# Expert 0's rows from a gather of six tiles and one-hot products of two, in a hybrid decoder layer with 32 experts

## The chip, the core and the metric

The kernel runs on one core of a Trainium2 chip. The metric is the device time of one execution, in microseconds. The engines are PE (TensorE, matrix products), DVE (VectorE), ACT (ScalarE), POOL (GpSimd) and SP (SyncE, which here only issues transfers). Each follows its own list of instructions in order; they meet at semaphores. The transfers of SP, ACT and POOL run on 16 shared DMA engines.

## The reference

The layer mixes tokens by a convolution group and an attention group, then runs a mixture of experts. The change is at the seam of the two:

```python
x = x + jnp.concatenate([yc, ya], axis=-1) @ w_out
xn = rms_norm(x, norm_ffn_w)
g_idx = argmax(xn @ w_group + b_group)            # 1 of 4 groups
top_v, top_i = top_k(e_logits of that group, 2)   # 2 of its 8 experts
# per expert e, over the tokens routed to it, in blocks:
h = silu(xb @ w1[e]) * (xb @ w3[e])
y = h @ w2[e]
x = x + sum over the token's two experts of gate * y
```

There are 1024 tokens of width 1024 and 32 experts of inner width 512. All is float32.

## The kernel before

**Tiles and stages.** The 1024 tokens are 8 tiles of 128, numbered m = 0 to 7. In the last loop of the mixing part PE multiplies tile m by `w_out` (`multiply`, halves h = 0 and 1 of 512 columns, eight chunks each), DVE adds the residual (`add(m, h)`), PE turns the sum (`turn`), ACT or DVE copies it out of PSUM, and PE multiplies it by the router's 36 columns (`route`). DVE then picks group and experts (`bias`, `choose_group`, `choose_experts`), PE counts how many earlier tokens chose each expert (`count_before`), and DVE makes from the count each token's slot in its expert's list (`rank`). `one_hots` on DVE and `table` on PE turn slots into a table of which token stands in which slot of which expert, by 16 products of one-hot matrices. DVE reads it with `slots`, which gives `slot_token`. Routing runs in groups of tiles: 0 to 3, 4 and 5, 6, 7. Normalised rows `xn2` of each tile are stored to DRAM by SP.

**Experts.** POOL gathers the rows of an expert, up to 128, from DRAM to `xg` (two buffers) by an indirect transfer. PE turns them (`pe_turn_x`; for expert 0 `first_turn_x`). ACT writes the rounded half `xT_hi`, DVE the rest `xT_lo`. Each weight matrix (`W1`, `W3`, `W2`: 2.1 MB each, two buffers of each, [0] for even experts and [1] for odd) is split the same way in four pieces: ACT writes `e_hi` (`act_split`), DVE `e_lo` (`dve_split`), and PE makes three products per chunk of the piece (`pe_product`). Six products of 512 columns belong to a piece, so 24 to a matrix. The order on PE for expert e is gate(e) with W1, the turn of the hidden values of e-1, up(e) with W3, the turn of the rows of e+1, down(e-1) with W2. Called "W3 of expert 2" below is the matrix that up(2) needs, in buffer `W3[0]`.

**What sets the order.** All orders are written out by hand. SP issues W3 of expert 0 when the last `multiply` is done, W1 of expert 1 when the first gather has landed, then W3 of expert 1, W2 of expert 0, W1 of expert 2, W2 of expert 1, and W3 of expert 2 when the split of W3 of expert 0 is done. Tokens over 128 for an expert go to a list of overflow blocks (`flag_blocks`, `list_blocks`, `listed`, `over_ready`), worked off at the end. Between the routing and the first expert PE runs 34 transposes whose result nobody reads (L1532, L1536).

## Time and profile before

| | us |
|---|---|
| median of 3 runs | 1164.63 |
| lowest, highest | 1163.91, 1165.25 |
| the profiled execution, its own time | 1164.24 |
| its span in the profile | 1162.1 |

| engine | busy us | share of the span |
|---|---|---|
| PE | 1096.3 | 94% |
| DVE | 900.1 | 77% |
| ACT | 718.6 | 62% |
| POOL | 139.7 | 12% |

The profile lists when each instruction started and what it waited for. The profiled execution took 0.39 us less than the median; its span leaves out 2.1 us around the work. The mixing part fills the span up to 530 us, the experts fill it from 550 us to some 1120 us, and the end reads the experts' results back and adds them.

### The profile page before, as it was taken

What the parts mean: (1) busy time and instruction counts of PE and PEld (TensorE: products, weight loads), DVE (VectorE), ACT (ScalarE), POOL (GpSimd) and SP (SyncE); (2) the same over time, 40 slices, a digit from 0 to 9 for tenths busy, and PEclk for the clock granted to TensorE, in tenths of its full rate; (3) what the DMA queues carried; (4) which work ended last, traced back from release to release, by engine and by line L of the source; (5) the groups of instructions that cost most, each with busy time, mean ns of one, the idle gap of its engine ahead of it and who ended that gap; (6) DMA issues with size and microseconds to landing.
All of it is one profiled execution on the core that took longest, in us unless ns stands there. A gap on an engine that the chain in (4) does not pass through costs nothing. (4 is left out here: it accounts for less than half of the span.)

```text
span 1162.1 us, 16798 instructions
## 1 busy us (share of the span) xinstructions
PE 1096.3 (94%) x5766; PEld 894.9 (77%) x5766; DVE 900.1 (77%) x1033; ACT 718.6 (62%) x882; POOL 139.7 (12%) x192
## 2 busy tenths in 40 slices
PE   8999999999999899997999999999999999999950
PEld 7887777778777668885878888888888888888840
DVE  5505957678575772567989999999999999999947
ACT  5423555646643571112878888888888888888830
POOL 1001000010000120001021110111111111101000
PEclk9999999999999999997999999999999999999985
DMA  7111231313213253003999999999999999999529
GB/s 232 46 35 39 90 89 59 107 39 107 67 46 95 103 214 142 37 37 133 425 427 422 396 384 396 386 384 396 382 383 390 382 392 383 390 387 387 214 77 375
DMA packets 77117, 275.29 MB, mean 237 GB/s; under 512 B 20752, under 2 KB 51600, under 8 KB 63888
## 3 DMA queue, kind: packets, MB, share of 16 engines
q1 hardware_dynamic: 66272, 253.69, 57.6%
q0 software_dynamic: 9216, 16.80, 3.8%
q10 hardware_dynamic: 1584, 4.20, 0.9%
q8 instruction: 29, 0.48, 0.2%
q14 instruction: 16, 0.13, 0.0%
HBM read 259.57 MB, written 31.85 MB: 251 GB/s over the span
## 5 line engine op out<-in xcount | busy, mean ns | idle before, releaser
L1198 DVE TENSOR_TENSOR e_lo<-W,e_hi 128x1024 fp32r<-128x1024 f32 x384 | 451.9, 1219 | 24.5 <-ACT e_hi L1192 21.7
L1192 ACT ACTIVATE e_hi<-W 128x1024 fp32r<-128x1024 f32 x384 | 403.4, 1060 | 94.7 <-PE ps L1163 88.7
L1161 PE MATMUL ps<-e_hi,xT_hi 128*128 128x512 f32 x496 | 196.3, 396 | 1.9 <-DVE xT_lo L1920 1.0
L1163 PE MATMUL ps<-e_lo,xT_hi 128*128 128x512 f32 x496 | 193.7, 390 | 0.0
L1162 PE MATMUL ps<-e_hi,xT_lo 128*128 128x512 f32 x496 | 193.1, 389 | 0.0
L472 PE MATMUL ps<-xnT_hi,w_hi 128*128 128x512 f32 x320 | 129.0, 403 | 1.6 <-DVE u L861 0.6
L472 PE MATMUL ps<-xnT_hi,w_lo 128*128 128x512 f32 x320 | 128.0, 400 | 0.0
L472 PE MATMUL ps<-xnT_lo,w_hi 128*128 128x512 f32 x320 | 125.3, 392 | 0.0
L900 DVE TENSOR_TENSOR_SCAN kept<-kept,start_at 128x1024 f32<-128x1024 f32 (+7 forms) x64 | 88.9, 1389 | 29.1 <-ACT kept L702 29.1
L1161 PEld LDWEIGHTS ps<-e_hi,xT_hi 128*128 128x128 f32 x496 | 93.5, 189 | 20.9 <-DVE xT_lo L1920 1.2
L1163 PEld LDWEIGHTS ps<-e_lo,xT_hi 128*128 128x128 f32 x496 | 93.1, 188 | 19.9
L1162 PEld LDWEIGHTS ps<-e_hi,xT_lo 128*128 128x128 f32 x496 | 93.3, 188 | 18.4
L1161 PE MATMUL ps<-e_hi,hidT_hi 128*128 128x512 f32 x256 | 102.4, 400 | 1.6 <-DVE hidT_lo L1232 1.6
L1163 PE MATMUL ps<-e_lo,hidT_hi 128*128 128x512 f32 x256 | 100.0, 390 | 0.0
L1162 PE MATMUL ps<-e_hi,hidT_lo 128*128 128x512 f32 x256 | 99.9, 390 | 0.0
L1259 POOL DMA_INDIRECT y_rows<-y,idx_pair x32 | 35.2, 1101 | 455.3 <-ACT y L1219 455.3
L711 ACT ACTIVATE probsT<-ps 128x512 f32<-128x512 f32 (+3 forms) x60 | 28.0, 504 | 84.1 <-PE ps L521 84.1
L472 PEld LDWEIGHTS ps<-xnT_hi,w_hi 128*128 128x128 f32 x320 | 60.1, 188 | 19.2 <-issue 7.1
L472 PEld LDWEIGHTS ps<-xnT_hi,w_lo 128*128 128x128 f32 x320 | 60.1, 188 | 13.0 <-issue 0.7
L472 PEld LDWEIGHTS ps<-xnT_lo,w_hi 128*128 128x128 f32 x320 | 60.1, 188 | 12.2 <-issue 0.5
L702 ACT ACTIVATE kept<-ps,q_minus 128x1024 f32<-128x1024 f32 (+7 forms) x64 | 47.8, 746 | 32.7 <-PE ps L510 32.6
L405 POOL CAST w_hi<-w_raw 128x1024 fp32r<-128x1024 f32 x20 | 22.4, 1120 | 301.4 <-DMA w_raw<-in_w_in_dram 301.4
(244 smaller groups left out, 1706.9 us busy)
## 6 DMA issues: line engine op xcount, KB each, us to landing
W<-in_w_dram SPq DMA_DIRECT2D x96, 2048.0 KB, 15.2
w_raw<-in_w_in_dram SPq DMA_DIRECT2D x20, 512.0 KB, 4.1
yy<-y_rows SPq DMA_DIRECT2D x7, 1024.0 KB, 12.7
xt<-in_x_dram SPq DMA_DIRECT2D x8, 512.0 KB, 3.7
w_out_raw<-in_w_out_dram SPq DMA_DIRECT2D x8, 512.0 KB, 6.4
xn_rows<-xn SPq DMA_DIRECT2D x8, 512.0 KB, 2.6
out_dram<-x ACTq DMA_DIRECT2D x7, 512.0 KB, 9.1
x<-in_x_dram SPq DMA_DIRECT2D x2, 1536.0 KB, 10.7
```

The lines of the kernel that those rows point to most:

```text
L405: pool.tensor_copy(w_hi[c % 2], w_raw[c % 2]).then_inc(w_hi_made, 1)
L472: mm = pe.matmul(ps[:, group_bank(g)], w, r, start=(i % TICKS == 0), stop=(i % TICKS == TICKS - 1))
L702: act.activation(kept[h][:, S - L:], z, ACT.Sigmoid, scale=down).then_inc(kept_made, 1)
L711: act.activation(probsT[h][:, k0:k1, :], TB(th(n, h) + hf)[:, 0:(k1 - k0) * P].rearrange("p (k t) -> p k t", t=P), ACT.Copy).then_inc(turn ...
L900: dve.tensor_tensor_scan(back, back, one[:, ::-1], 0.0, ALU.mult, ALU.max).then_inc(multiplied, 1)
L1161: pe.matmul(o, xs_hi[:, k], e_hi[:, p, cols], start=(k == 0), stop=False)
L1162: pe.matmul(o, xs_lo[:, k], e_hi[:, p, cols], start=False, stop=False)
L1163: mm = pe.matmul(o, xs_hi[:, k], e_lo[:, p, cols], start=False, stop=(k == last))
L1192: act.activation(e_hi[:, p], flat[:, p * D:(p + 1) * D], ACT.Copy).then_inc(s["hi_made"], 1)
L1198: dve.tensor_tensor(e_lo[:, p], flat[:, p * D:(p + 1) * D], e_hi[:, p], ALU.subtract).then_inc(s["lo_made"], 1)
L1259: pool.indirect_dma_start(out=y_rows, out_offset=bass.IndirectOffsetOnAxis(ap=idx_pair[b].bitcast(U32), axis=0), in_=y[b], in_offset=None, ...
```

## The change

Expert 0 no longer waits for the whole table. Four things are done:

1. **Expert 0's rows.** `rank` also makes `first_code`, a token's place in expert 0's list plus one, or zero. `first_one_hots` makes from it a one-hot matrix for each tile (`HOT(m)`). For tiles 0 to 5 `first_list` multiplies these by the tokens' numbers, and POOL gathers the rows named while tile 7 is still multiplied. ACT and DVE split the rows (`first_hi`, `first_lo`), and `first_gathered` turns them by products with the identity `eye`. For tiles 6 and 7 no row is gathered: `first_added` multiplies the normalised rows, still in SBUF, by the tile's one-hot matrix into the same PSUM banks. `first_turn_x` and the 34 unread transposes are gone.
2. **Weights of expert 0's gate.** W1 of expert 0 is split during tiles 5 to 7 into buffers of its own, `e0_hi` and `e0_lo`.
3. **The last half tile.** The second half of tile 7 is added, turned, copied and routed as two parts of 256 columns (`add_last`, `turn_last`, `route_last`). Its second `scale_last` now stands ahead of `bias`.
4. **Order behind.** The last four products of the table stand inside the gate of expert 0, ahead of its last piece. The overflow list stands inside up(0), and the turn of expert 1's rows behind up(0). SP issues W1 of expert 1 right behind the last store of rows, and W3 of expert 1 once expert 1's rows have been gathered.

The core of the diff:

```diff
+HOT = lambda m: first_hot[:, m] if m < NT - 2 else last_hot[:, m - NT + 2]
+first_hi = at("first_hi", 136, [P, D], F32R)
...
-def act_split(act, s, start, w, pieces=range(PIECES)):
+def act_split(act, s, start, w, pieces=range(PIECES), hi=e_hi, free=False):
...
+        if not free:
+            act.wait_ge(s["freed"], start + p + 1)
+        act.activation(hi[:, p], flat[:, p * D:(p + 1) * D], ACT.Copy).then_inc(s["hi_made"], 1)
...
@@ -1333,8 +1351,8 @@
                 sp.dma_start(W3[0], w3_v[0]).then_inc(expert_w[0][1], 16)
             sp.wait_ge(xn2_made, m + 1 if m < NT - 1 else NT + 1)
             sp.dma_start(xn2_rows_v[m], xn2[m % 2]).then_inc(xn2_stored[m % 2], 16)
-        sp.wait_ge(s_e["gathered"][0], 16)
         sp.dma_start(W1[1], w1_v[1]).then_inc(expert_w[1][0], 16)
+        sp.wait_ge(s_e["gathered"][1], 16)
         sp.dma_start(W3[1], w3_v[1]).then_inc(expert_w[1][1], 16)
...
+        sp.wait_ge(s_e["freed"], used(gate_start(0) + PIECES))
         load(W1, w1_v, 2, 0, 0, gate_start(0))
...
         for b in range(2):
-            pool.wait_ge(xn2_stored[b], 16 * (NT // 2))
+            pool.wait_ge(xn2_stored[b], 16 * (NT // 2 - 1))
+        pool.wait_ge(first_listed, 1)
+        gather_rows(pool, xg[0], first_token, s_e["gathered"][0], S - 2 * P)
+        pool.wait_ge(xn2_stored[0], 16 * (NT // 2))
+        pool.wait_ge(xn2_stored[1], 16 * (NT // 2))
         pool.wait_ge(routed, 1)
-        for e in range(2):
-            gather_rows(pool, xg[e], slot_token[:, e:e + 1], s_e["gathered"][e])
+        gather_rows(pool, xg[1], slot_token[:, 1:2], s_e["gathered"][1])
         pool_gather(pool, s_e, 2, 0, 1, 1, 2)
         pool_gather_start(pool, s_e, 0, 1)
...
+        def turn_last():
+            for q in range(2):
+                pe.wait_ge(x2_made, 2 * NT + q)
+                pe.wait_ge(x2T_made, 2 * NT - 2 + q)
+                for k in range(2):
+                    c = 4 + 2 * q + k
+                    mm = pe.transpose(ps[:, 5 - q, k * P:(k + 1) * P], x2[:, X2(NT - 1), c * P:(c + 1) * P], ident)
+                mm.then_inc(x2_turned, 1)
...
+        def route_last():
+            for q in range(2):
+                pe.wait_ge(x2T_made, 2 * NT + q)
+                for k in range(4 + 2 * q, 6 + 2 * q):
+                    mm = pe.matmul(ps[:, 6, P:P + LOG], x2T[1][:, k], router_w[:, k], start=False, stop=(k == KT - 1))
...
+        def first_list():
+            bank, c0 = FIRST_AT
+            pe.wait_ge(iotas, 12)
+            pe.wait_ge(first_hots, NT - 2)
+            for m in range(NT - 2):
+                mm = pe.matmul(ps[:, bank, c0:c0 + 2], first_hot[:, m], token_less[:, m:m + 2], start=(m == 0), stop=(m == NT - 3))
+            mm.then_inc(first_summed, 1)
...
+        def first_gathered(h):
...
+                pe.wait_ge(rows0_lo_made, 1)
+                pe.wait_ge(x2_made, 2 * NT + 1)
+            for k in range(4 * h, 4 * h + 4):
+                o = psf[:, k * P:(k + 1) * P]
+                pe.matmul(o, first_hi[:, k:D:KT], eye, start=(k % 4 == 0), stop=False)
+                pe.matmul(o, first_lo[:, k:D:KT], eye, start=False, stop=False)
+
+        def first_added(m, ks):
+            if ks[0] == 0:
+                pe.wait_ge(first_hots, m + 1)
+                pe.wait_ge(xn2_made, m + 1 + (m == NT - 1))
+            for k in ks:
+                mm = pe.matmul(psf[:, k * P:(k + 1) * P], xn2[m % 2][:, k:D:KT], HOT(m), start=False, stop=(m == NT - 1 and k % 4 == 3))
+                if m == NT - 1 and k % 4 == 3:
+                    mm.then_inc(s_e["turned"] if k == KT - 1 else half_turned, 1)
...
+            if m == 7:
+                first_list()
...
             multiply(pe, m, 1, (4, 5))
-            if m == 7:
-                route(7, 0)
-                count_before(2)
-            multiply(pe, m, 1, (6, 7))
             if m == 6:
                 count_before(1)
...
+            if m == 7:
+                count_before(2)
+                route(7, 0)
+            multiply(pe, m, 1, (6, 7))
...
+        turn_last()
+        first_gathered(0)
+        route_last()
+        first_gathered(1)
+        first_added(NT - 2, range(0, KT - 1))
         count_before(3)
         count_all()
-        table(12, 16)
-        for i in range(20):
-            pe.transpose(ps[:, 4, 0:P], ident, ident)
-        pe.wait_ge(listed, 1)
-        pe.matmul(ps[0:1, 3, 0:P], over_col, ident, start=True, stop=True).then_inc(list_turned, 1)
-        for i in range(14):
-            pe.transpose(ps[:, 4, 0:P], ident, ident)
...
+        first_added(NT - 2, (KT - 1,))
+        first_added(NT - 1, range(KT))
...
             pe.wait_ge(half_lo_made, 1)
-            pe_product(pe, s_e, 0, xT_hi, xT_lo, [ps[:, 2]], 2, KT - 1, (0, 1))
+            pe_product(pe, s_e, 0, xT_hi, xT_lo, [ps[:, 2]], 2, KT - 1, (0, 1), **own)
             pe.wait_ge(s_e["xT_made"], 1)
-            pe_product(pe, s_e, 0, xT_hi, xT_lo, [ps[:, 2]], 2, KT - 1, (2, 3))
+            pe_product(pe, s_e, 0, xT_hi, xT_lo, [ps[:, 2]], 2, KT - 1, (2,), **own)
+            table(12, 16)
+            pe_product(pe, s_e, 0, xT_hi, xT_lo, [ps[:, 2]], 2, KT - 1, (3,), **own)
...
+                pe_product(pe, s_e, up_start(0), xT_hi, xT_lo, [ps[:, 3]], 2, KT - 1, (0, 1))
+                overflow_list()
+                pe_product(pe, s_e, up_start(0), xT_hi, xT_lo, [ps[:, 3]], 2, KT - 1, (2, 3))
+                pe_turn_x(pe, s_e, 1, 1, 1)
+                return
+            if isinstance(e, int) and e == 1:
                 pe.wait_ge(over_ready, 1)
-                pe_turn_x(pe, s_e, 1, 1, 1)
...
+                if m == NT - 2:
+                    act.wait_ge(s_e["gathered"][0], 16)
+                    act.activation(first_hi, xg[0], ACT.Copy).then_inc(rows0_hi_made, 1)
...
+                    act.wait_ge(y_lo_made, Y_PARTS)
+                    act.wait_ge(expert_w[0][0], 16)
+                    act_split(act, s_e, gate_start(0), W1[0], hi=e0_hi, free=True)
...
+            act_split(act, s_e, up_start(e), W3[b], free=isinstance(e, int) and e == 0)
             if isinstance(e, int) and e == 0:
+                act.wait_ge(s_e["freed"], used(gate_start(0) + PIECES))
                 act_xT(act, s_e, 1)
...
+        def add_last():
+            dve.wait_ge(mixed, 2 * NT)
+            for q in range(2):
+                cols = slice(BANK // 2 * q, BANK // 2 * (q + 1))
+                part = x2[:, X2(NT - 1), BANK:][:, cols]
+                dve.tensor_tensor(part, MB(NT - 1, 1)[:, cols], part, ALU.add).then_inc(x2_made, 1)
...
+        def first_one_hots(first, last):
+            for m in range(first, last):
+                dve.tensor_scalar(HOT(m), iota[:, 1:P + 1], first_code[:, m:m + 1], None, ALU.is_equal).then_inc(first_hots, 1)
...
+            link(dve.scalar_tensor_tensor(first_code[:, ms], earlier[:, :, 0], 1.0, chosen[:, ms, 0], ALU.add, ALU.mult))
+            if i == 3:
+                first_one_hots(NT - 1, NT)
...
-                rank(1)
                 one_hots(8, 12)
+                dve.wait_ge(first_summed, 1)
+                dve.tensor_scalar(first_token, ps[:, FIRST_AT[0], FIRST_AT[1]:FIRST_AT[1] + 1], 2.0 * S, None, ALU.add).then_inc(first_listed, 1)
+                dve_split(dve, s_e, gate_start(0), W1[0], (2,), hi=e0_hi, lo=e0_lo)
...
                 choose_experts(1)
+                rank(1)
+                first_one_hots(4, 6)
             if m == 7:
                 choose_experts(2)
+                dve.wait_ge(rows0_hi_made, 1)
+                dve.tensor_tensor(first_lo, xg[0], first_hi, ALU.subtract).then_inc(rows0_lo_made, 1)
                 rank(2)
-            add(m, 1)
+                first_one_hots(6, 7)
+            if m == NT - 1:
+                add_last()
...
+            if m == 6:
+                dve_split(dve, s_e, gate_start(0), W1[0], (1,), hi=e0_hi, lo=e0_lo)
...
-
-        dve.wait_ge(x2_turned, 2 * NT)
-        dve.tensor_copy(x2T[1][:, 4:8].rearrange("p k t -> p (k t)"), ps[:, 5]).then_inc(x2T_made, 1)
-        one_hots(12, 14)
+            if m == 5:
+                first_one_hots(0, 4)
+                dve_split(dve, s_e, gate_start(0), W1[0], (0,), hi=e0_hi, lo=e0_lo)
...
+        for q in range(2):
+            dve.wait_ge(x2_turned, 2 * NT + q)
+            dve.tensor_copy(x2T[1][:, 4 + 2 * q:6 + 2 * q].rearrange("p k t -> p (k t)"), ps[:, 5 - q, 0:BANK // 2]).then_inc(x2T_made, 1)
         invert(NT - 1)
         scale_last(0)
+        scale_last(1)
         bias(NT - 1)
         choose_group(3)
         choose_experts(3)
-        scale_last(1)
         rank(3)
+        one_hots(12, 14)
+        first_x_lo()
+        dve_split(dve, s_e, gate_start(0), W1[0], (3,), hi=e0_hi, lo=e0_lo)
         one_hots(14, 16)
-        dve.wait_ge(table_step, HOTS)
-        slots(slice(0, NE))
...
             if isinstance(e, int) and e == 0:
-                dve_split(dve, s_e, gate_start(0), W1[0], (2, 3))
+                dve_split(dve, s_e, up_start(0), W3[0], (0, 1))
+                pick_blocks()
+                dve_split(dve, s_e, up_start(0), W3[0], (2,))
+                list_blocks()
+                dve_split(dve, s_e, up_start(0), W3[0], (3,))
                 make_gates()
-            elif not (isinstance(e, int) and e == 1):
-                dve_split(dve, s_e, gate_start(e), W1[b])
-            dve_split(dve, s_e, up_start(e), W3[b])
-            if isinstance(e, int) and e == 0:
+                dve_split(dve, s_e, gate_start(1), W1[1], (0,))
                 dve_xT(dve, s_e, 1)
-                dve_split(dve, s_e, gate_start(1), W1[1], (0, 1))
+                dve_split(dve, s_e, gate_start(1), W1[1], (1,))
                 dve_hid(dve, s_e, 0, up_start(0))
                 dve_split(dve, s_e, gate_start(1), W1[1], (2, 3))
...
+        ask_gates()
         flag_blocks()
+        dve.wait_ge(table_step, HOTS)
+        slots(slice(0, NE))
```

**PE, from the counts of tile 7 to the first product of an expert.** Before:

```order
L1481 MATMUL ps<-chosen,ones 128x32 x7
L1486 MATMUL ps<-chosen,ones 128x32 x8
L1492 MATMUL ps<-of_column_162,of_slot_158 128x256 [waits hot]
L1492 MATMUL ps<-of_column_163,of_slot_159 128x256 [waits hot]
L1492 MATMUL ps<-of_column_164,of_slot_160 128x256 [waits hot]
L1492 MATMUL ps<-of_column_165,of_slot_161 128x256 [waits hot]
L1532 MATMUL ps<-start_at 128x128 x20
L1534 MATMUL ps<-start_at,over_col 1x128 [waits listed]
L1536 MATMUL ps<-start_at 128x128 x14
L1542 MATMUL ps<-start_at,xg_183 128x128 [waits first_gathered0]
L1542 MATMUL ps<-start_at,xg_183 128x128 x7
L1161 MATMUL ps<-e_hi,xT_hi 128x512 [waits first_lo_made,half_lo_made]
```

After (`xn_0`, `xn_1` are the normalised rows of tiles 6 and 7):

```order
L1553 MATMUL ps<-eye,first_lo 128x128
L1560 MATMUL ps<-last_hot,xn_0_96 128x128 [waits xn2_made,first_hots]
L1560 MATMUL ps<-last_hot,xn_0_96 128x128 x6
L1521 MATMUL ps<-chosen,before 128x32 [waits chosen_made,iotas]
L1523 MATMUL ps<-chosen,ones 128x32 x7
L1528 MATMUL ps<-chosen,ones 128x32 x8
L1560 MATMUL ps<-last_hot,xn_0_96 128x128
L1560 MATMUL ps<-last_hot,xn_1_97 128x128 [waits xn2_made,first_hots]
L1560 MATMUL ps<-last_hot,xn_1_97 128x128 x7
L1179 MATMUL ps<-e_hi,xT_hi 128x512 [waits first_lo_made,half_lo_made]
```

The table's products, the unread transposes, the overflow list and the turn of gathered rows are gone from this place; 15 products with the one-hot matrices of tiles 6 and 7 stand there, around the counts. The eight of tile 7 wait for its one-hot matrix.

**PE, between gate(0) and gate(1), around the turn of expert 1's rows.** Before, the turn stands between gate(0) and up(0):

```order
L1163 MATMUL ps<-e_lo,xT_hi 128x512
L1150 MATMUL ps<-start_at,xg_184 128x128 [waits first_xT_made,first_gathered1,over_ready]
L1150 MATMUL ps<-start_at,xg_184 128x128 x7
L1161 MATMUL ps<-e_hi,xT_hi 128x512 [waits first_lo_made,first_hidden]
L1162 MATMUL ps<-e_hi,xT_lo 128x512
```

After, it stands between up(0) and gate(1):

```order
L1181 MATMUL ps<-e_lo,xT_hi 128x512
L1168 MATMUL ps<-start_at,xg_188 128x128 [waits first_xT_made,first_gathered1]
L1168 MATMUL ps<-start_at,xg_188 128x128 x7
L1179 MATMUL ps<-e_hi,x1T_hi 128x512 [waits first_lo_made,first_silu,first_xT_made]
L1180 MATMUL ps<-e_hi,x1T_lo 128x512
```

The product behind the turn needs, in the order before, rows that were turned long ago (`xT_hi`), and in the new order the very rows just turned (`x1T_hi`).

**SP, weights from the last `multiply` on.** `W_0_102` is buffer W1[0], `W_0_104` W3[0], `W_0_106` W2[0]; `W_1_103`, `W_1_105` and `W_1_107` are W1[1], W3[1] and W2[1]. Before:

```order
L1333 DMA W_0_104<-in_w_dram 128x4096 [waits mixed]
L1335 DMA xn_rows<-xn_1_97 128x1024 [waits xn2_made]
L1337 DMA W_1_103<-in_w_dram 128x4096 [waits first_gathered0]
L1338 DMA W_1_105<-in_w_dram 128x4096
L1341 DMA W_0_106<-in_w_dram 128x4096 [waits list_turned,listed]
L1346 DMA W_0_102<-in_w_dram 128x4096 [waits first_lo_made]
L1350 DMA W_1_107<-in_w_dram 128x4096
L1346 DMA W_0_104<-in_w_dram 128x4096 [waits first_lo_made]
```

After:

```order
L1351 DMA W_0_104<-in_w_dram 128x4096 [waits mixed]
L1353 DMA xn_rows<-xn_1_97 128x1024 [waits xn2_made]
L1354 DMA W_1_103<-in_w_dram 128x4096
L1356 DMA W_1_105<-in_w_dram 128x4096 [waits first_gathered1]
L1359 DMA W_0_106<-in_w_dram 128x4096 [waits list_turned,listed]
L1364 DMA W_0_102<-in_w_dram 128x4096 [waits first_lo_made,first_freed]
L1369 DMA W_1_107<-in_w_dram 128x4096
L1364 DMA W_0_104<-in_w_dram 128x4096 [waits first_lo_made]
```

W1 of expert 1 (third row) waits for no gather any more; W3 of expert 1 and all behind it wait for the gather of expert 1's rows.

## Rows read from the trace of the kernel before

**Rows 1.** PE waits from 530 us to the end: total, times, longest.
```profile
PE ps L1479 <- DVE chosen L1774: 4.2, 1, 4.2
...
PE ps L1161 <- DVE e_lo L1198: 1.0, 1, 1.0
```

**Rows 2.** PE timeline: start, length, engine, line, operation, count, [idle before <-releaser].
```profile
516.15 0.60 PE L1458 MATMUL ps<-start_at,x 128*128 128x128 f32 x4
...
529.78 0.40 PE L1312 MATMUL ps<-w_out_hi,yT_lo 128*128 128x512 f32 x1
...
532.47 1.51 PE L1468 MATMUL ps<-router_w,x2T 128*128 128x36 f32 x8 [0.78 <-DVE x2T L1849]
538.19 0.18 PE L1479 MATMUL ps<-chosen,before 128*128 128x32 bf16 x1 [4.21 <-DVE chosen L1774]
...
541.70 4.47 PE L1532 MATMUL ps<-start_at 128*128 128x128 f32 x20
...
548.30 1.16 PE L1542 MATMUL ps<-start_at,xg 128*128 128x128 f32 x8
550.43 0.50 PE L1161 MATMUL ps<-e_hi,xT_hi 128*128 128x512 f32 x1 [0.97 <-DVE xT_lo L1920]
...
551.00 0.39 PE L1163 MATMUL ps<-e_lo,xT_hi 128*128 128x512 f32 x1
...
555.78 0.40 PE L1163 MATMUL ps<-e_lo,xT_hi 128*128 128x512 f32 x1
```

**Rows 3.** PE timeline: start of expert 1 gate, and of expert 2 up.
```profile
563.26 0.47 PE L1161 MATMUL ps<-e_hi,x1T_hi 128*128 128x512 f32 x1 [0.73 <-issue]
...
588.15 0.47 PE L1161 MATMUL ps<-e_hi,xT_hi 128*128 128x512 f32 x1 [0.96 <-DVE e_lo L1198]
```

**Rows 4.** ACT timeline: the splits that waited for a weight transfer.
```profile
559.24 2.01 ACT L1192 ACTIVATE e_hi<-W 128x1024 fp32r<-128x1024 f32 x2 [1.05 <-DMA W<-in_w_dram]
...
565.26 2.08 ACT L1192 ACTIVATE e_hi<-W 128x1024 fp32r<-128x1024 f32 x2 [0.20 <-DMA W<-in_w_dram]
...
585.69 3.90 ACT L1192 ACTIVATE e_hi<-W 128x1024 fp32r<-128x1024 f32 x4 [2.40 <-DMA W<-in_w_dram]
```

**Rows 5.** SP timeline: issues of W1 of expert 1 and of the last normalised rows.
```profile
538.73 0.32 SPq L1335 DMA_DIRECT2D xn_rows<-xn  x1
548.27 0.33 SPq L1337 DMA_DIRECT2D W<-in_w_dram  x1
```

**Rows 6.** Windows: PE, PEld, DVE, ACT, POOL busy; PEclk, DMA share, GB/s.
```profile
540.00:542.00 2.00, 1.20 (x4) 0.97 (x5) 1.29 (x6) 0.00 (x0) 0.00 (x0) 0.50 0.41 168
...
546.00:548.00 2.00, 2.00 (x16) 1.47 (x16) 1.97 (x6) 0.00 (x0) 0.85 (x1) 0.85 0.36 113
...
570.00:575.00 5.00, 5.00 (x25) 4.16 (x24) 4.87 (x6) 3.78 (x6) 0.00 (x0) 1.00 1.00 428
```

**Rows 7.** DVE timeline: ranking of tiles 4 and 5, then the end of the routing.
```profile
518.22 0.47 DVE L1784 TENSOR_TENSOR ranked<-ps,of_expert 128x64 f32<-128x64 f32 x2
...
520.06 0.29 DVE L1797 TENSOR_SCALAR of_slot<-iota,slot 128x128 fp32r<-128x128 f32 x1
...
534.23 0.25 DVE L1717 SCALAR_TENSOR_TENSOR logits<-ps,rr,router_b 128x36 f32<-128x36 f32 x1
...
537.85 0.19 DVE L1774 TENSOR_TENSOR chosen<-of_expert 128x32 bf16<-128x32 f32 x1
...
541.94 0.19 DVE L1803 TENSOR_SCALAR unused<-ps 128x32 f32<-128x32 f32 x1 [0.68 <-PE ps L1492]
```

**Rows 8.** POOL timeline, and the tile view of the gathers from 540 us.
```profile
543.66 1.46 POOL L1244 DMA_INDIRECT xg<-xn_rows,slot_token  x1 [38.90 <-issue]
...
DMA to landing us min/median/max: 4.6/11.6/14.9
```

**Rows 9.** PE timeline elsewhere: one true f32 product of 512 columns (two records).
```profile
303.81 1.10 PE L488 MATMUL ps<-k_sq,same_head 128*128 128x512 f32 x2
```

**Rows 10.** ACT timeline: table load before the first silu.
```profile
561.26 1.28 ACT L1214 ACT_TABLE_LOAD   x1
```

112 lines of the change are left out of this document (68 added, 44 removed).

## The prediction

> **What bounds the kernel now.** First the list of PE's waits from 530 us on: some 10 us in 570, and only two places matter here, 4.2 us for the choice of experts of the last tile and 1.0 us for a split piece of weights [rows 1]. Then the timeline of PE in the seam [rows 2]: the last product with `w_out` starts at 529.78 and ends at 530.17, the first product of expert 0 starts at 550.43. These 20.3 us hold only routing, a gather and 34 unread transposes. From 550.43 PE stands still twice: 0.7 us ahead of gate(1) at 563.26, and 1.0 us ahead of up(2) at 588.15 [rows 3]. The second stop asks for the other half of the reading, the transfers. ACT waited for a weight matrix 1.05 us until 559.24, when W1 of expert 1 landed, and 2.4 us until 585.69, when W3 of expert 2 did; the last is what PE stood still for [rows 4]. Six matrices had to come between the landing of the first gather at 548.27, when SP could issue again, and 585.69 [rows 4, 5]: 6 x 2.1 MB at 428 GB/s [rows 6] are 29.4 us of the 37.4, the rest is start, gathered rows and what is queued behind. So there are **two chains** through the seam: PE's own, with 1.0 us of slack at up(2), and that of the transfers, with none. After up(2) PE runs without a stop, so the time at which up(2) starts is the time of the whole kernel. What counts of a gain at the start of expert 0 is what reaches up(2).
>
> **Part 1: until the last product with `w_out`.** `rank(1)` moves ahead of `add(6, 1)`. It is eight small operations in 1.84 us, from 518.22 to the one-hot at 520.06, to which come a `first_code` (0.2) and two one-hots at the spacing of 0.20 us [rows 7]: 2.45 us and the 0.7 of the addition behind counts that now stand ahead of the last six products of tile 6, ready at about 513.3, so the addition ends at 516.5 where PE had taken it at 516.15 [rows 2]: +0.4. `first_list` puts six products in PE's way. The router's products take 1.51 us for eight records at half clock, 0.19 each [rows 2]; at full clock half of that, so six cost 0.6 (ends 0.6 and 1.1). The gather of six tiles can start when DVE has the list, about 521.9, behind eight one-hots of the table that now start at 519.5. From the read of the table at 541.94 the old gather needed 1.7 us to its start at 543.66, of which 0.6 were reads that are gone, and 4.6 us more to land [rows 7, 8]: 521.9 + 1.1 + 4.6 = 527.6. ACT splits the rows in 1.0 us and only then copies out the turned first half of tile 7, which the router wants on PE at 528.8 and gets at 529.2: +0.4. Together the last product ends at **531.6** in place of 530.17, +1.5 (ends +0.5 and +3). The four early pieces of W1 lie in holes of ACT and DVE between the tiles, and I put them at nothing; if a hole is missed, a piece costs DVE 1.2 us.
>
> **Part 2: to the choice of experts for tile 7.** From the last product's end to the router's last four products it took 2.3 us [rows 2], addition, turn and copy one behind the other; in two overlapping parts that is worth 0.3. But eight products with `eye` now stand ahead of the router's last four, both `scale_last` (0.75 each) stand ahead of `bias`, and they need the root of a square that starts after the whole addition: `bias` at 535.75 instead of 534.23. The row of 14 small operations behind it is unchanged, 3.8 us [rows 7], so the choice is ready at **539.55** and not at 538.04.
>
> **Part 3: to the first product of expert 0.** Before: choice, counts, rank, table, gather, turn, 12.4 us. Now: counts 0.55, `first_code` 0.2, one-hot 0.3, then eight true f32 products of 128 columns. The nearest row is a true f32 product of 512 columns: two records of 0.43 us spacing (1.10 us for both with the tail of the last, 0.16) [rows 9]. A quarter of it is 0.21 us at full and 0.43 at half clock: 1.7 or 3.4 us for eight, from 540.7. DVE is busy with the rest of `rank` and two pairs of one-hots to 542.85, then subtracts the half. From the turn at 548.30 to the first product took 2.13 us with one half turned, copied and subtracted [rows 2], some 1.6 behind the half. So expert 0 starts at 543.6 (full) to 544.4 (half); I take **543.9**, 6.5 us earlier than before.
>
> **The clock.** PE's granted clock was 0.50, the lower level of 1.2 GHz, at 540 us, after PE had stood still 4.2 us for the choice; it rose to 2.4 GHz within the stretch 546 to 548 (mean 0.85), behind several us in which the unread transposes filled PE [rows 2, 6]. The change takes these 34 away, and PE stands still from about 537 to 539.6 for the choice. I take half clock for most of the eight products and 0.3 us lost in the gate. The Trainium skill (TensorE: Matmul & The Clock Gate, "What's actually happening") says that the throttled state is the default and that activity releases it; by that rule the filler was worth its place, and the rows agree so far.
>
> **Part 4: to the transfers.** The table's last products now stand behind three pieces of the gate: 18 products at 0.2275 us (551.00 to 555.78 are 21 of them [rows 2]) are 4.1, with 0.3 for the clock and 0.6 for the four: the table ends at 548.9, where it had ended at 541.9. From there the way is the old one, `slots`, gather, landing: 541.94 to 548.27 is 6.3 us [rows 5, 7]. So W3 of expert 1 is issued at **555.3**, and all weights behind it, 7.0 us later than SP could go on before. In exchange W1 of expert 1 comes in the quiet time behind the store of the rows, from about 536 to 543: one matrix of the six is out of the way, 2.1 MB at 428 GB/s = 4.9 us [rows 6]. Some 0.2 us more for rows gathered before. Landing of W3 of expert 2, and start of up(2): +7.0 - 4.9 - 0.2 = **+1.9 us**. The gather is priced with idle transfer engines, 4.6 us to landing; amid the weight stream the median was 11.6 [rows 8]. The Trainium skill (DMA: Bandwidth & Descriptors, "Queues, rings and completion order") says each engine takes turns between its queues packet by packet; by it a gather beside W1 of expert 1 would land late, but that matrix should be through.
>
> **Part 5: PE's own chain.** In up(0) PE now waits for DVE, which does `flag_blocks`, `slots`, `pick_blocks` and `list_blocks` between the pieces (about 3.5 us). The turn of expert 1's rows, once hidden ahead of up(0), now stands right before gate(1): turn 0.9, copy 1.0, two pieces 2.0, table load 1.28 [rows 10], silu 0.6 lie bare. Counting on, gate(1) starts at about 564.8 against 563.26: +1.5. Less the 1.0 us that PE waits at up(2) anyway: +0.5, which is hidden behind the +1.9 of the transfers. Waits in gate(1) and up(1) I put at nothing; DVE and ACT are a piece ahead there.
>
> **The sum.** 1164.24 + 1.9 = 1166.1 against the profiled execution. It lay 0.4 below the median of the three runs, so against the median the forecast is 1164.63 + 1.9 = **1166.5 us**. A measurement of this kernel tells about 0.2% (2.3 us) from no change, so this is within that.
>
> **Rivals.** (a) *PE stays at half clock through the gate.* Each of the 18 products ahead of the table then costs 0.2 us more, up to 3.6, and every one delays the table, the gather and the weights. It decides from two to three such products: 1.9 + 0.2 x 2.5 passes 2.3 us. With eight to 16 products slow the time is 1168.1 to 1169.7. For it: 0.50 at 540 in spite of work on PE [rows 6]; against it: the f32 products that run from 540.7. (b) *The early gather lands late* (beside stores, or behind a slower issue): ACT's copy and DVE's addition stand behind it, so each us is a us: +2 gives 1168.5. (c) *The transfers are not the bound*: W3 of expert 2 lands earlier than my sum since the queue is shorter, and the choice comes as early as before, so that expert 0 starts at 541.5. Then PE's chain decides, 3 us better than in part 5: +0.5 - 3 = -2.5, some 1162.1. Against it: bytes and rate leave little [rows 6], and 541.5 is the floor, since the choice at 538.04 plus 3.5 us must be passed. (d) *The whole 6.5 us reach the end*, 1158.1: this needs the transfers to gain as much, against part 4.
>
> **How the numbers follow.** That the sum holds to within its own ends, +0.3 to +2.3 and now and then below, has 0.54, and all of it is within 0.2%. (a) 0.26 and (b) 0.11 are slower; (c) 0.07 and (d) 0.02 are faster. Faster 0.09, same 0.54, slower 0.37. The range leaves out (d), most of (c) and the far end of (a): 1163.2 to 1169.3.
>
> **What would show it.** Right: first product of expert 0 at 543 to 545; the last `w_out` product near 531.6; W1 of expert 1 issued near 536, W3 of expert 1 at 554 to 557, with idle transfer engines in between; gate(1) within 2 us of 563.3; a wait of 1 to 3 us at up(2) for a weight transfer. Wrong: up(2) starting before 587, which would mean that the transfers keep the gain; clock 0.50 until 548 or later, which is (a); the copy of the early rows on ACT later than 529, which is (b).

## The result

| us | before | after |
|---|---|---|
| median | 1164.63 | 1168.91 |
| runs, lowest and highest | 7 runs, 1161.61 to 1166.65 | 7 runs, 1167.52 to 1169.81 |
| span of the profiled execution | 1162.1 | 1166.6 |

The ratio of after to before is 1.0037, with a 95% interval of 1.0025 to 1.005. The forecast was 1166.5, within a range of 1163.2 to 1169.3. The time is in the range, but the likeliest case (within 0.2%) was wrong: the kernel is slower by 0.37%, and its time is 2.4 us above the forecast.

### The profile page after: what moved, and what is told of

Read it like the earlier page. It is cut to its first block and busy times, and to the rows that moved or that the text cites. A ratio compares the mean times of both kernels' runs of the same rounds, so it can differ in the third digit from the quotient of the medians.

```text
span 1166.6 us, 16847 instructions
## 1 busy us (share of the span) xinstructions
PE 1102.3 (94%) x5778; PEld 901.1 (77%) x5778; DVE 905.3 (78%) x1049; ACT 719.1 (62%) x883; POOL 137.9 (12%) x195
## 5 line engine op out<-in xcount | busy, mean ns | idle before, releaser
L1179 PEld LDWEIGHTS ps<-e_hi,xT_hi 128*128 128x128 f32 x496 | 93.5, 189 | 20.9 <-DVE e_lo L1216 2.8
L1277 POOL DMA_INDIRECT y_rows<-y,idx_pair x32 | 32.6, 1020 | 457.1 <-ACT y L1237 457.1
```

Of the source, the lines that this page charges most:

```text
L1179: pe.matmul(o, xs_hi[:, k], hi[:, p, cols], start=(k == 0), stop=False)
L1277: pool.indirect_dma_start(out=y_rows, out_offset=bass.IndirectOffsetOnAxis(ap=idx_pair[b].bitcast(U32), axis=0), in_=y[b], in_offset=None, ...
```

## The profile after

PE's waits from 500 us to the end (total, times, longest), which answer to [rows 1]:

```profile
PE ps L1179 <- ACT act_out L1232: 5.0, 1, 5.0
PE ps L1179 <- DVE hidT_lo L1250: 1.6, 1, 1.6
PE ps L1179 <- DVE e_lo L1216: 1.6, 3, 0.8
```

The 4.2 us for the last choice of experts are gone and so is the 1.0 us at up(2). In their place stands one wait of 5.0 us. The timeline of PE says where (start, length, engine, line, operation, count, [idle before <-releaser]); it answers to [rows 2, 3]:

```profile
527.02 0.72 PE L1534 MATMUL ps<-of_column,of_slot 128*128 128x256 f32 x4
...
531.29 0.40 PE L1330 MATMUL ps<-w_out_hi,yT_lo 128*128 128x512 f32 x1
532.20 0.77 PE L1492 MATMUL ps<-start_at,x 128*128 128x128 f32 x4 [0.52 <-DVE x L1783]
532.72 0.43 PE L1552 MATMUL ps<-eye,first_hi 128*128 128x128 f32 x1
532.99 0.40 PE L1553 MATMUL ps<-eye,first_lo 128*128 128x128 f32 x1
533.22 0.40 PE L1552 MATMUL ps<-eye,first_hi 128*128 128x128 f32 x1
...
537.48 3.55 PE L1560 MATMUL ps<-last_hot,xn 128*128 128x128 f32 x14
540.87 0.18 PE L1521 MATMUL ps<-chosen,before 128*128 128x32 bf16 x1
...
541.27 4.60 PE L1560 MATMUL ps<-last_hot,xn 128*128 128x128 f32 x18
545.63 0.47 PE L1179 MATMUL ps<-e_hi,xT_hi 128*128 128x512 f32 x1
...
559.93 1.05 PE L1168 MATMUL ps<-start_at,xg 128*128 128x128 f32 x8
566.00 0.76 PE L1179 MATMUL ps<-e_hi,x1T_hi 128*128 128x512 f32 x1 [5.02 <-ACT act_out L1232]
566.56 0.63 PE L1180 MATMUL ps<-e_hi,x1T_lo 128*128 128x512 f32 x1
566.99 0.63 PE L1181 MATMUL ps<-e_lo,x1T_hi 128*128 128x512 f32 x1
...
573.86 0.63 PE L1197 MATMUL ps<-start_at,hid 128*128 128x128 f32 x4
...
591.62 0.63 PE L1197 MATMUL ps<-start_at,hid 128*128 128x128 f32 x4
592.01 0.48 PE L1179 MATMUL ps<-e_hi,xT_hi 128*128 128x512 f32 x1
```

Three things are to be seen. From 532.7 PE has no stop that would end in an idle remark until gate(1), apart from three short ones in up(0), yet expert 0 starts only at 545.63: the products with `eye` follow each other every 0.24 us, and the 18 records of the one-hot products take 4.60 us. Then the stop of 5.02 us ahead of gate(1). And behind it the products stand 0.43 us apart, not 0.23, which is half clock. The windows of PE (length, PE busy, granted clock as a share of 2.4 GHz, DMA share, GB/s) show the fall inside the wait:

```profile
562.00:564.00 2.00, 0.00 (x0) 1.00 0.96 393
564.00:566.00 2.00, 0.00 (x0) 0.52 0.98 418
566.00:568.00 2.00, 2.00 (x5) 0.50 1.00 422
568.00:570.00 2.00, 2.00 (x7) 0.50 1.04 440
570.00:572.00 2.00, 2.00 (x8) 0.77 1.01 428
```

The clock had fallen once before, and there without a stop longer than the 0.52 us at 532.20. PE was busy by the profile in every one of these microseconds, with the `eye` products and those of tile 6:

```profile
536.00:538.00 2.00, 2.00 (x9) 0.69 1.06 434
538.00:540.00 2.00, 2.00 (x11) 0.50 0.88 320
```

The same fall, between 534 and 540 us, stands in all six executions shown here that have these products in this form, and in none of the five in which they stand closer together (experiment 2). Why it falls there is not shown. It costs next to nothing, since these products keep their pace at either clock.

ACT's timeline has the cause of the wait, and no wait for a weight transfer any more (compare [rows 4, 10]):

```profile
561.08 1.02 ACT L1221 ACTIVATE x1T_hi<-ps 128x1024 fp32r<-128x1024 f32 x1 [7.34 <-PE ps L1168]
562.00 1.99 ACT L1210 ACTIVATE e_hi<-W 128x1024 fp32r<-128x1024 f32 x2
564.01 1.28 ACT L1232 ACT_TABLE_LOAD   x1
565.30 0.60 ACT L1232 ACTIVATE act_out<-ps 128x512 f32<-128x512 f32 x1
```

ACT had stood idle for 7.34 us until PE had turned expert 1's rows. Only then come copy, two pieces, table load and sigmoid product (the `silu` of expert 0), one behind the other, and gate(1) waits for the last. The sigmoid product needed neither the copy nor the pieces: gate(0) had long been done. DVE was not far behind: it had `x1T_lo`, the other half of the copied rows, ready at 565.51.

The time can be booked on PE's own line. The two turns of hidden values that bound gate(1) and up(2) stand, in before, here:

```profile
568.81 0.63 PE L1179 MATMUL ps<-start_at,hid 128*128 128x128 f32 x4
...
586.56 0.63 PE L1179 MATMUL ps<-start_at,hid 128*128 128x128 f32 x4
```

| us | before | after | difference |
|---|---|---|---|
| ninth table product | 525.61 | 527.02 | +1.41 |
| from there to gate(1) | 37.65 | 38.98 | +1.33 |
| gate(1) to the turn behind it | 5.55 | 7.86 | +2.31 |
| from that turn to the next | 17.75 | 17.76 | +0.01 |
| from there to up(2) | 1.59 | 0.39 | -1.20 |
| start of up(2) | 588.15 | 592.01 | **+3.86** |

What is left to the difference of the spans, 0.6 us, lies behind up(2). From up(2) to the end took 573.4 to 574.7 us in the thirteen executions shown here: 573.95 and 573.45 in the two kernels with the old design, 574.1 to 574.7 in after and its five relatives with strided rows, and 573.4 to 573.7 in the five executions with contiguous rows (experiment 2). What makes these differences is not shown. The runs below are compared by the distance from the table row (the ninth table product, called the eighth tile's first in the expectations; L1492 in the old design, L1533 or L1534 in the new) to up(2), since the table row itself lay anywhere from 526.9 to 528.5 in the six kernels that are the same up to it. The +1.41 of the first row is thus one draw from +1.3 to +2.9. Each distance comes from one execution; the one kernel that was profiled twice had 17.52 and 17.28 to expert 0, 58.96 and 58.75 to up(2), so differences of 0.2 us mean nothing.

## Experiments

The theory that the trace suggests (A): PE's own chain decides, by the late expert 0, the bare row on ACT and the clock that falls in the wait. The rival (B) is the prediction's: the transfers decide.

**1. Filling the wait.** After, with unread transposes in the wait before gate(1).

```diff
                         pe_turn_x(pe, s_e, 1, 1, 1)
+                        for i in range(48):
+                            pe.transpose(ps[:, 4, 0:P], ident, ident)
                         return
```

> The changed kernel with 48 unread transposes on PE between the turn of expert 1's rows and gate(1), where PE stood still for 5.0 us and then ran 12 products of gate(1) at half clock. Theory A (PE's own chain sets the end, and the fallen clock is part of its price): the clock stays at 1.00, the 12 products cost 0.23 us each and not 0.43, the start of gate(1) stays, the time falls by 2.3 us to about 1166.6. Theory B (the weight transfers set the end, as forecast): PE arrives earlier at up(2) and waits there, the time stays at 1168.9.

Measured 1167.12 us, ratio 1.0027 (1.0014 to 1.004). The windows of PE, as above:

```profile
562.00:564.00 2.00, 2.00 (x20) 1.00 0.96 410
564.00:566.00 2.00, 2.00 (x21) 1.00 1.03 442
566.00:568.00 2.00, 2.00 (x11) 1.00 1.01 428
```

Gate(1) starts at 565.93, where it had been, but the turn behind it comes at 571.50, not 573.86, and up(2) is 62.71 us from the table row, not 64.99. So the 2.3 us in the table are the clock's, and nothing else took their place. The proof is the trace: the interval of the times overlaps that of after, and of the ten runs six lie at 1165.2 to 1167.3 us and four at 1168.9 to 1169.9, where those of after lie. The transfers were early enough for an up(2) 2.3 us earlier, which (B) did not allow.

**2. The columns of one weight tile side by side.** The stationary side of the `eye` and one-hot products took every eighth column of a row (`k:D:KT`). Here the normed rows are written chunk by chunk, so that it is contiguous. The turns of gathered rows (L1168) are changed in the same way.

```diff
-                        pe.matmul(o, first_hi[:, k:D:KT], eye, start=(k % 4 == 0), stop=False)
+                        pe.matmul(o, first_hi[:, k * P:(k + 1) * P], eye, start=(k % 4 == 0), stop=False)
...
-                    dve.scalar_tensor_tensor(xn2[b], x2[:, X2(m)], ...)
+                    dve.scalar_tensor_tensor(xn2[b].rearrange("p (k t) -> p t k", k=KT), by_k(x2[:, X2(m)]), ...)
```

> The changed kernel with the normalised rows written in chunk-major order, so that all products that load 128 columns of them as the stationary operand read them without a stride (before: every eighth element). Theory A: the stride is why the loads of the eye and one-hot products take 0.337 us and the products come every 0.24 us; without it loads take 0.19 and products come every 0.09 to 0.11 us at full clock, expert 0 starts about 2 us earlier (543.6), time about 1166.9. Rival: a non-transposing float32 product of 128 columns costs 0.24 us whatever the layout; then spacing and time stay. Writing in that order may cost DVE more per tile; the trace shows it.

Measured 1167.45 us, ratio 1.0027 (1.0015 to 1.004). First the tile view of PE's weight loads in after (count; shortest, median, longest in ns; first and last start; form), then the same line in this kernel:

```profile
L1552 PEld LDWEIGHTS ps<-eye,first_hi x8: 312/337/338, 532.7 to 536.9; 128*128 128x128 f32 x8
L1499 PEld LDWEIGHTS ps<-router_w,x2T x8: 189/192/208, 534.6 to 535.4; 128*128 128x128 f32 x8
```

```profile
L1552 PEld LDWEIGHTS ps<-eye,first_hi x8: 190/192/193, 534.5 to 536.9; 128*128 128x128 f32 x8
```

And from its PE timeline:

```profile
534.75 0.28 PE L1552 MATMUL ps<-eye,first_hi 128*128 128x128 f32 x1
534.87 0.27 PE L1553 MATMUL ps<-eye,first_lo 128*128 128x128 f32 x1
534.98 0.27 PE L1552 MATMUL ps<-eye,first_hi 128*128 128x128 f32 x1
```

The spacing falls from 0.24 to 0.11 us, the load from 337 to 192 ns, so the rival (0.24 us whatever the layout) is out. The one-hot products of tile 6 take 1.77 us instead of 3.55. In the turns of gathered rows, which are transposes and not true products, the loads fall from 188 to 140 ns and the mean record only from 273 to 272 ns. The bill comes on DVE, which now writes each row in steps of 128 floats. Its groups by line, in after and then here (count, busy us, mean ns):

```profile
L1793 DVE SCALAR_TENSOR_TENSOR xn<-x,rr,g2b 128x1024 f32<-128x1024 f32 x7 | 9.0, 1285 | 0.2
```

```profile
L1794 DVE SCALAR_TENSOR_TENSOR xn<-x,rr,g2b 128x1024 f32<-128x1024 f32 x7 | 14.4, 2055 | 0.2
```

The scaling of a tile costs 2.06 us instead of 1.29, the last choice comes later, and PE waits 2.9 us for it. In that wait the clock falls (0.51 in 542 to 544). Of 3.8 us saved on PE ahead of the counts (16 x 0.126 = 2.0, and 1.8) the distance from the table row to expert 0 shows 0.7: 17.89 us, not 18.61. The Trainium skill (Advanced Engine Details and Errata, "SBUF Cachelines") says that accesses that go to a new 16-byte line each time are slowed; the loads' steps of eight floats and the writes' of 128 both do that, and both measurements agree in direction.

**3. ACT's order.** The sigmoid product with its table load and the first two pieces of gate(1) ahead of the copy of expert 1's rows, and on DVE both pieces ahead of its half of these rows.

```diff
-                        act.wait_ge(s_e["freed"], used(gate_start(0) + PIECES))
-                        act_xT(act, s_e, 1)
+                        act_silu(act, s_e, 0, gate_start(0))
                         act.wait_ge(expert_w[1][0], 16)
                         act_split(act, s_e, gate_start(1), W1[1], (0, 1))
-                        act_silu(act, s_e, 0, gate_start(0))
+                        act_xT(act, s_e, 1)
...
-                        dve_split(dve, s_e, gate_start(1), W1[1], (0,))
+                        dve_split(dve, s_e, gate_start(1), W1[1], (0, 1))
                         dve_xT(dve, s_e, 1)
-                        dve_split(dve, s_e, gate_start(1), W1[1], (1,))
```

> The changed kernel with silu(0), its table load and the first two pieces of gate(1) on ACT ahead of the copy of expert 1's turned rows, and with the subtraction of these rows on DVE behind both pieces, which are then ready. Theory A (PE's chain): of the 5.0 us wait at gate(1) the copy and the subtraction stay, 2.4 us; gate(1) starts at 563.4 and not 566.0, and if the clock then stays up, 2.3 us more are won: 1164.3 to 1166.5. Theory B (transfers): a wait for a weight matrix appears at up(2) and the time stays within 1 us of 1168.9.

Measured 1166.59 us, ratio 1.002 (1.0011 to 1.003). Gate(1) now waits 2.37 us, and comes 36.33 us from the table row, not 38.98. But up(2) is at 63.08, 1.9 us better, where 2.65 us had been won at gate(1) alone. The clock fell again, so gate(1) to the turn took 7.21 us, and from the second turn to up(2) it took 1.79 us, not 0.39. PE's line and then ACT's timeline tell who took the rest:

```profile
591.17 0.47 PE L1179 MATMUL ps<-e_hi,xT_hi 128*128 128x512 f32 x1 [1.15 <-DVE e_lo L1216]
```

```profile
567.65 1.06 ACT L1210 ACTIVATE e_hi<-W 128x1024 fp32r<-128x1024 f32 x1 [2.65 <-DMA W<-in_w_dram]
...
588.70 3.91 ACT L1210 ACTIVATE e_hi<-W 128x1024 fp32r<-128x1024 f32 x4 [2.59 <-DMA W<-in_w_dram]
```

Here the transfers are the bound, just behind PE's chain, and the fallen clock may have cost nothing more: without it PE would, by this trace, have waited longer at up(2). Each theory had one of its signs. This run also measures the prediction's other chain: W3 of expert 2 is split at 588.70, less 1.07 for the later table row (528.09 against 527.02) 587.6, against 585.69 in [rows 4]. That is +1.9 us, the forecast's own figure (its terms are compared below).

**4. The transfer alone.** After, with W3 of expert 1 issued right behind its W1, at 537.34 instead of 556.49.

```diff
-                sp.wait_ge(s_e["gathered"][1], 16)
                 sp.dma_start(W3[1], w3_v[1]).then_inc(expert_w[1][1], 16)
```

> The changed kernel with W3 of expert 1 issued right behind W1 of expert 1, not behind the gather of expert 1's rows: one more matrix in the quiet time of the transfer engines. Theory A (PE's chain sets the end): nothing, 1168.9. Theory B (transfers set the end): 2 to 4 us less. If the gather of the rows of expert 1 is caught behind the transfer, it lands later than at 556.4 and PE's chain grows.

Measured 1168.62 us, ratio 1.0041 (1.0026 to 1.0055): the 5.0 us wait and half clock stay, and up(2) is 64.73 us from the table row, 0.3 less, where (B) wanted 2 to 4. In after the transfers do not bind, and (B) falls.

**5. Both, and the old kernel's transfers.** Edits 3 and 4 together:

> After, with both edits: the table load, the sigmoid product of expert 0 and the first two hi pieces of gate(1) ahead of the copy of expert 1's rows on ScalarE, and the load of W3 of expert 1 right behind that of W1. Theory (with the order of ScalarE mended the transfers become the bound, which the early load frees): ScalarE's waits for weights, 5.8 us in the run with the first edit alone, fall below 1 us, the distance from the eighth tile's first table product to up(2) goes from 63.08 to about 61.0, and the time is 1164.6 (ratio 1.000), 2 us under the first edit alone. Rival (the early load is worth nothing, as when it was made alone): 1166.6 again. Rival (TensorE's waits for e_lo, 2.6 us, are VectorE's own pace and not that of the weights): half of the gain, 1165.6.

Measured 1165.90 us (10 runs, 1163.04 to 1166.40), ratio 1.0012 (1.0001 to 1.0022). ACT has no wait for a weight matrix left, and up(2) comes at 60.27 us, 4.7 us earlier than in after and 0.7 earlier than expected; the time is 1.3 us above the 1164.6 expected. Against experiment 3 up(2) comes 2.8 us earlier. Of the wait for the transfers, 1.4 us are gone (0.39 from the second turn to up(2), not 1.79), and 1.6 us are the clock's (5.58 from gate(1) to the turn, not 7.21), less 0.2 by which gate(1) came later: with the same wait of 2.37 us the granted clock stayed up. The window 566 to 568 in experiment 3 and here:

```profile
566.00:568.00 2.00, 2.00 (x6) 0.50 0.99 420
```

```profile
566.00:568.00 2.00, 2.00 (x10) 1.00 0.97 418
```

Why it fell once and not the other time is not shown. Had it fallen here too, the early transfer would have brought some 1.2 us (an estimate, 2.8 less 1.6). In the ratios (1.002 and 1.0012) the two kernels cannot be told apart.

In the old kernel, W1 of expert 1 ahead of the wait for the first gather:

```diff
-                sp.wait_ge(s_e["gathered"][0], 16)
                 sp.dma_start(W1[1], w1_v[1]).then_inc(expert_w[1][0], 16)
+                sp.wait_ge(s_e["gathered"][0], 16)
```

> Before, with the load of W1 of expert 1 issued ahead of the wait for the first gather, so that it starts about 536 instead of 543 and the transfers behind it can all start earlier. Theory of the prediction (two chains end at up(2), the transfers' with no slack, TensorE's own with 1.0 us): ScalarE's waits for weights before gate(1) and up(2) [1.05 and 2.40 us] go, up(2) starts about 1.0 us earlier, at 587.2, and the time is 1163.6 (ratio 0.999). Rival (TensorE's own chain has no slack either): up(2) at 588.1 as in before, the time within 0.3 us of 1164.6. Rival (the early load takes bandwidth from the gathers of both experts' rows): first turn of expert 0's rows later than 548.3, 1165 or more.

Measured 1165.24 us, ratio 1.0004 (0.9993 to 1.0015). ACT's waits for weights vanish and up(2) follows the turn without a stop:

```profile
549.01 1.16 PE L1542 MATMUL ps<-start_at,xg 128*128 128x128 f32 x8 [0.71 <-DMA xg<-xn_rows,slot_token]
...
587.35 0.48 PE L1161 MATMUL ps<-e_hi,xT_hi 128*128 128x512 f32 x1
```

It is 61.47 us from the table row, not 62.54. From the second turn to up(2) PE won 1.20 us, the slack of its chain that the prediction had read off [rows 3]. The turn of expert 0's rows had to wait 0.71 us for its gather, whose engines were busy in a share of 0.94 in 544 to 546 where it had been 0.14; expert 0 starts 0.43 us later from the table row, and 0.13 of that is left at gate(1), which makes 1.07. The time itself shows no gain that can be told (1163.6 was expected), so the slack stands by the trace alone.

**6. The same with a filler, and with contiguous rows.** Edits 3 and 4 and 24 transposes as in 1:

> The same two edits, and 24 transposes that nobody reads between the turn of expert 1's rows and gate(1). Theory (what is left of the clock's fall is worth about 1 us, twelve products or fewer at half clock): granted clock 1.00 in gate(1), 0.5 to 1.0 us under the kernel with the two edits, 1163.8. Rival (the wait of 2.4 us before gate(1) is too short to cost the clock much, or the transposes delay gate(1) by what they win): within 0.2 us of the kernel with the two edits. What stands against before after all of that is the later start of expert 0's product and the wait of 2.4 us.

Measured 1164.51 us, ratio 1.0001 (0.9991 to 1.0011). In the trace the transposes bring nothing (60.22 against 60.27 us, where the theory wanted 0.5 to 1.0), since the clock had not fallen at gate(1) without them; the lower median is not explained by them. With edit 2 as well:

> The two edits and the 24 transposes, and the normed rows written so that the columns of one weight tile lie side by side. Theory (eye products at 0.11 us instead of 0.24 save 3.4 us of TensorE, of which VectorE's dearer scaling, 2.05 instead of 1.29 us a tile, leaves about 0.7 us): distance from the eighth tile's first table product to the first product of expert 0 17.9 us instead of 18.6, 0.7 us under the kernel without this, 1163.1, which would be under before. Rival (the scaling also delays the last choice and the row stores, and the second gather with them): no gain or a loss of up to 1 us against the kernel without it.

Measured 1162.71 us, ratio 0.9987 (0.9977 to 0.9996); 58.96 us to up(2), 1.3 less. To expert 0 it is 17.52 us, 1.2 less where edit 2 alone had won 0.7: there the 18 records behind the choice had taken 3.83 us at a fallen clock, here 2.58. The same kernel once more:

> The kernel with two edits, 24 transposes and contiguous rows once more, unchanged, beside the next one and with more rounds, since its lead over before (0.13 per cent) is near what three rounds tell. Expected: 1162.7 again, ratio 0.9985 to 0.999. Rival (the lead was the scatter of one chip's runs): ratio 0.9995 or more.

Measured 1162.33 us, ratio 0.9987 (0.9977 to 0.9996) again; 17.28 us to expert 0 and 58.75 to up(2).

**7. DVE's order, and the other wait.** In that kernel PE waited 1.1 us for `xT_lo`, and DVE did two one-hot pairs of the table first:

```diff
-                one_hots(12, 14)
                 first_x_lo()
+                one_hots(12, 14)
```

> The kernel with two edits, 24 transposes and contiguous rows, and with VectorE's one-hot tiles of the table's steps 12 and 13 (1.0 us) behind the remainder of expert 0's rows instead of ahead of it. Theory (VectorE is the bound of the seam there: in that kernel TensorE waited 1.1 us for xT_lo, and the first xT_hi had been ready at about 544.6 while xT_lo started at 545.15): the distance from the eighth tile's first table product to expert 0's first product goes from 17.5 to 16.9 us, 0.5 us in time against the same kernel without the edit. Rival (the late one-hot tiles make TensorE wait at the table instead, or the second half of xT_hi, ready at 545.4, is the bound): within 0.2 us of it.

Measured 1162.24 us, ratio 0.9982 (0.997 to 0.9993). Expert 0 starts 16.83 us from the table row, not 17.3 to 17.5, but its first products run at half clock, and up(2) comes at 59.17, no better than 58.75 to 58.96. The 18 one-hot records took 3.50 us. PE's windows:

```profile
542.00:544.00 2.00, 2.00 (x13) 0.58 1.09 467
544.00:546.00 2.00, 2.00 (x7) 0.57 1.02 426
```

The clock had fallen after the wait of 2.9 us for the choice. In both executions of the kernel without this edit it had stayed at 1.00 behind the same wait. So that wait was filled too:

```diff
+                for i in range(20):
+                    pe.transpose(ps[:, 4, 0:P], ident, ident)
                 count_before(3)
```

> The kernel with the one-hot tiles behind the remainder, and 20 more transposes that nobody reads in TensorE's wait of 2.9 us for the last tile's choice. In the kernel without them the nine one-hot products behind that wait (18 records) took 3.5 us instead of 2.1 and the first gate products began at half clock, so that expert 0's product started 0.45 us earlier than in the kernel with the one-hot tiles ahead, but up(2) came 0.4 us later, counted from the table row (59.17 against 58.75). Theory (the clock fell in that wait): granted clock 1.00 from 530 to 550, up(2) at about 58.2 us from the table row, 1161.4 us. Rival (the clock was fallen for another reason, or the transposes hold up the counts): clock 0.5 to 0.6 in 542 to 546 as before, 1162.2 or more.

Measured **1160.77 us**, ratio 0.9972 (0.9962 to 0.9982), faster than before. The 18 records took 2.57 us, and the same windows read:

```profile
542.00:544.00 2.00, 1.35 (x9) 1.00 0.95 401
544.00:546.00 2.00, 2.00 (x10) 1.00 1.03 434
```

Up(2) is 58.21 us from the table row, where 58.2 was expected: 1.0 us less than in the run before, for the clock, the cause that experiment 1 had shown. The intervals of the two ratios overlap, so this 1.0 us too stands by the trace.

Each ratio is taken to runs of before on the same chip, whose medians were 1164.1 to 1164.3 us beside the experiments, so the times of two rows are not to be subtracted. Nor does a shorter distance alone make a faster kernel: the table row came at 525.6 and 525.9 us in the two kernels with the old design and at 526.5 to 528.5 in all others. That is why up(2) is 2.3 us nearer in "order, W3" than in before and the time is not.

| kernel | us | ratio to before | table row to expert 0, gate(1), up(2) |
|---|---|---|---|
| before | 1164.63 | 1 | 24.82, 37.65, 62.54 |
| after | 1168.91 | 1.0037 | 18.61, 38.98, 64.99 |
| filler | 1167.12 | 1.0027 | 18.61, 39.00, 62.71 |
| contiguous | 1167.45 | 1.0027 | 17.89, 38.26, 64.77 |
| ACT's order | 1166.59 | 1.002 | 18.61, 36.33, 63.08 |
| W3 early | 1168.62 | 1.0041 | 18.74, 39.11, 64.73 |
| order, W3 | 1165.90 | 1.0012 | 18.82, 36.54, 60.27 |
| order, W3, filler | 1164.51 | 1.0001 | 18.75, 36.48, 60.22 |
| the same, contiguous | 1162.71 | 0.9987 | 17.52, 35.24, 58.96 |
| the same, one-hots later | 1162.24 | 0.9982 | 16.83, 35.49, 59.17 |
| the same, two fillers | 1160.77 | 0.9972 | 16.66, 34.52, 58.21 |
| before, W1 early | 1165.24 | 1.0004 | 25.25, 37.78, 61.47 |

## Why the prediction was right or wrong

That the time lies in the range is luck as far as the mechanism goes. The sum made the transfers decide, at +1.9 us; PE's own chain decided, at +3.9 at up(2), and the range reached so far up only for the sake of rivals (a) and (b), of which neither happened.

**Part 1 and 2 held, in part by luck.** The last `w_out` product ended at 531.7 (531.6 forecast), the early rows' copy started at 527.09 and was done by 528.2 (not later than 529), `bias` ran at 535.74 (535.75), and the choice was ready at 539.56 (539.55). DVE's timeline:

```profile
535.74 0.25 DVE L1807 SCALAR_TENSOR_TENSOR logits<-ps,rr,router_b 128x36 f32<-128x36 f32 x1
...
539.37 0.19 DVE L1864 TENSOR_TENSOR chosen<-of_expert 128x32 bf16<-128x32 f32 x1
```

At the table row itself the change had cost 1.41 us where the same terms gave 1.0, and the way from there to the last product cost 0.1 more where 0.4 stood for the copy on ACT. Since the table row varies by 1.6 us between kernels that are the same up to it, agreement to 0.1 us in one execution is chance.

**Part 3 failed, by 1.7 us.** The choice was ready on time but PE took it at 540.87, since it was still at the products of tile 6: the sixteen products with `eye` and the one-hot products of tile 6 had been put at nothing, as if they filled a wait. And the nine products behind it (nine, not eight: the last chunk of tile 6 is moved there) took 4.60 us at nearly full clock, 0.48 each from start to start, where a quarter of a 512-column product [rows 9] gave 0.21. The seven products of tile 6, run mostly at half clock (0.50 in 538 to 540), had the same 0.48 each. The quarter scales the columns that stream through; these products, whose pace doesn't change with the granted clock, go by the loading of their strided weights, which the chosen row did not contain. With contiguous ones, experiment 2 has 0.25 a product at full clock with the tail (14 records in 1.77 us), near the quarter. The trace of before had no true product with such a load; a bound from above should have been kept in the sum.

**The clock was looked for in the wrong place.** Around the gate of expert 0 it was back at 0.95 in 540 to 542 us, earlier than forecast, and rival (a) did not happen. It had fallen at 536, with PE at work and not in the stop that was forecast from 537 to 539.6, and the stop did not come. What cost time was the fall at gate(1).

**Part 4 held, as a chain that does not decide.** W1 of expert 1 was issued at 536.02 (536), and W3 of expert 1 at 556.49 (555.3, as the table came late), with idle transfer engines between. SP's timeline, which answers to [rows 5]:

```profile
536.02 0.43 SPq L1354 DMA_DIRECT2D W<-in_w_dram  x1
556.49 0.33 SPq L1356 DMA_DIRECT2D W<-in_w_dram  x1
```

Its +1.9 us at up(2) is what experiment 3 laid bare, though not by the forecast's terms: W3 of expert 1 was issued 8.2 us later than SP could go on before, not 7.0, so what came in exchange was worth some 6.3 us and not 5.1 (an estimate from 8.2 and 1.9). The forecast wait of 1 to 3 us at up(2) did not come, since PE was later still.

**Part 5 is the step that failed.** It had every operation of the bare row ahead of gate(1), and the sum was near: 20.9 us from expert 0's start to gate(1) forecast, 20.4 measured. It then counted gate(1) itself at its old length. A stop of PE of about 5 us follows from its own numbers, and [rows 2, 6] show half clock behind one of 4.2 us. That makes +2.31 us which stood in no term; the wait in gate(1) had been put at nothing and its length left alone. In PE's chain, the forecast had +1.5 at gate(1), less 1.0 at up(2), so +0.5. Measured are +2.74 at gate(1), +2.31 for the clock, less 1.20: +3.86, twice the transfers' +1.9. The other 1.2 us at gate(1) are part 3's 1.7 less 0.5. Rival (c), PE's chain deciding, was priced only for a gain; that it could decide by being late was missed. The Trainium skill (TensorE: Matmul & The Clock Gate, "What's actually happening") has the rule that was quoted for the early filler and not applied here: without activity the array is throttled. Experiments 1 and 7 agree with it, 2.3 and 1.0 us. The fall at 536 us, with PE busy by the profile, is not explained by the rule as it was quoted.

**Rivals (b) and (d)** did not occur: the early gather landed about 4.1 us after its issue at 523.01, and of the 4.8 us by which expert 0 started earlier nothing reached the end in after.

## What to carry to other kernels

When a piece of work is moved out of a wait, list what had lain in that wait for free and where it lies now; here it was a copy, a table load and a sigmoid product, and their order on ACT and DVE alone held gate(1) up by 2.65 us of the 4.8 that expert 0 had won. A new stop of TensorE of a few microseconds can have a second price behind it, what runs next at half clock, and it belongs into the sum beside the stop: it was 2.3 us behind a stop of 5.0, and behind stops of 2.4 and 2.9 it came in some executions and not in others. And where two chains are within 2 us of each other, an edit that frees one of them measures as nothing until the other is freed: the early transfer gave 0.3 us of distance alone, and behind the new order 2.8, of which 1.6 hung on the clock.
